# An expert layer with 96 slots on four 32-column groups of TensorE and fp32 weights that are not split

## The chip, the cores and the metric

The kernel runs on one core of a Trainium2 chip. The metric is the device time of one execution in microseconds; lower is better. The profiled execution's time and its span (first to last recorded instruction) are both given below. TensorE is called PE, its weight loads PEld, VectorE DVE, ScalarE ACT, and the queue that issues the weight transfers SP.

## What is computed

The model has two layers over 256 tokens (128 of a prompt and 128 latent). Layer 0 ends in a dense feed-forward block; layer 1 ends in eight experts of which each token uses two. D_MODEL is 1024, D_FF_EXPERT is 3584, and everything is float32.

```python
def swiglu(h, w_gate, w_up, w_down):
    return (jax.nn.silu(h @ w_gate) * (h @ w_up)) @ w_down

def moe_swiglu(h, w_router, we_gate, we_up, we_down):
    ...
    top_v, top_i = lax.top_k(logits, TOP_K)
    top_w = jax.nn.softmax(top_v, axis=-1)
    gates = jnp.sum(jax.nn.one_hot(top_i, N_EXPERTS, dtype=jnp.float32) * top_w[..., None], axis=1).astype(h.dtype)
    y = jnp.zeros_like(x)
    for e in range(N_EXPERTS):
        y = y + gates[:, e:e + 1] * swiglu(x, we_gate[e], we_up[e], we_down[e])
    return y.reshape(b, s, d)
```

One expert's three matrices hold 3 x 1024 x 3584 floats, 44.04 MB, and all eight experts are read.

## The kernel before

The layers ahead of the experts (modulation, projections, attention, pooling, dense block, router) are the same in both kernels and take the first 580 us. Then a loop, written once and run eight times on every engine, does one expert per pass.

**Slots.** The tokens of an expert are put into 128 slots by a matmul with a 0/1 matrix P (`gather`, into the tile xg), and its outputs Y are spread back over the 256 tokens and weighted by a matmul with PgT (`combine`), which DVE adds to the result (`add_up`). If an expert had more tokens than slots, a second round would follow under an `If`; with this data no expert has over 77 tokens.

**Weights.** SP loads the weights in items of 1 MB into `ring`, 7 slots of 8 KB in each of 128 partitions; an expert has 42 items. Gate and up items are 4 rows of 512 columns (2 KB each) in a partition, down items one row of 8 KB. ACT copies each half item (a piece) into `high`, rounded to the type fp32r, and DVE puts the difference into `low`; each piece is then used in three matmuls instead of one (high times high, high times low, low times high). An fp32r matmul is one hardware matmul; a plain fp32 call is two, each with its own weight load, so that a call appears in the trace as two MATMUL and two LDWEIGHTS records. The transposes are one each.

**Steps.** The 3584 hidden columns are done in 7 steps of 512. A step is `into_hidden(0, ...)` for gate (24 matmuls of 512 columns), `turn` of the step before (4 transposes), `into_hidden(1, ...)` for up (24), and `down` of the step before (24). In all an expert has 504 fp32r matmuls of 128x128 by 512 columns, 28 transposes, a gather (16 calls) and a combine (8 calls).

**Order.** Every engine has a program of its own, in the order of the code, and they meet at semaphores: SP waits for `low_ready` before it loads into a slot, ACT waits for `in_slot` and `pieces_used`, DVE for `high_ready`, PE for `low_ready`. Silu is one ACT instruction over 512 columns, the product with up one of DVE.

**Four column groups elsewhere.** The modulation (`mod_rows`, L1222) already uses 32-column matmuls on the four 32-column groups of the array, in plain fp32: eight calls, call i into partitions 32i to 32i+31 of one bank, each with its own 512 weight columns streaming:

```python
                    for i in range(4):
                        k = 4 * half + i
                        last = mm(mod_rows_of(m)[32 * i:32 * i + 32, :], silu_c[:, k, :], w[:, i, :], start=half == 0, stop=half == 1)
```

Of the kernel before, what the change touches and what calls it, by code (L numbers as in the profile page):

```python
# [18 lines left out]
D = 1024  # L19
# [14 lines left out]
NE = 8  # L34
FE = 3584
# [12 lines left out]
EC = 512  # L48
ESTEPS = FE // EC
# [4 lines left out]
E_ITEMS = 6 * ESTEPS  # L54
E_PIECES = 2 * E_ITEMS
assert E_PIECES % PIECES == 0
COMBINE_BANKS = (6, 7, 3, 2)
# [126 lines left out]
MOE_ARRIVED = list(_count)  # L184
PER_EXPERT = [len(range(s, E_ITEMS, SLOTS)) for s in range(SLOTS)]

# [4 lines left out]
def piece_g(c):  # L191
    return 0 if c == 0 else 12 * c - 4


def piece_u(c):
    return piece_g(c) + 4


def piece_d(c):
    return 12 * c + 16 if c < ESTEPS - 1 else E_PIECES - 4  # L200


def expert_item(i):

    for c in range(ESTEPS):
        for what, at in (("g", piece_g(c)), ("u", piece_u(c)), ("d", piece_d(c))):
            if 0 <= 2 * i - at < 4:
                return what, c, (2 * i - at) // 2


def program(nc, ins, consts, y_prompt, y_sample, new_ckv, new_kpe):
# [10 lines left out]
    with ctx:  # L222
# [10 lines left out]

        ring = sb("ring", 128, SLOTS, SLOT)
        high = sb("high", 128, PIECES, PIECE, dt=f32r)
        low = sb("low", 128, PIECES, PIECE, dt=f32r)
        cst = sb("cst", 128, C_COLS)
# [67 lines left out]
        hTm = sb("hTm", 128, 2, EC // 128, 128, dt=f32r)  # L305
        xg = sb("xg", 128, 2, KD, 128, dt=f32r)
        ehid = sb("ehid", 128, 2, 2, EC)
        sg, hm = ehid[:, 0], ehid[:, 1]
        h2 = sb("h2", 128, 2, D)
        P = sb("P", 128, NE + 1, 2, 128)  # L310
        PgT = sb("PgT", 128, NE + 1, 2, 128)
        Y = sb("Y", 128, D)
        Pg = sb("Pg", 128, NE, 2, 128)
# [5 lines left out]
        in_slot = [sem(f"in_slot{i}") for i in range(SLOTS)]  # L319
# [23 lines left out]
        esg_ready, eh_ready, ehT_done, ehTh_ready, ehT_ready = (sem(x) for x in ("esg_ready", "eh_ready", "ehT_done", "ehTh_ready", "ehT_ready"))  # L343
        Y_ready, cmb_done, acc_ready = sem("Y_ready"), sem("cmb_done"), sem("acc_ready")
        gat_done, xgh_ready, xg_ready = sem("gat_done"), sem("xgh_ready"), sem("xg_ready")
# [64 lines left out]
        TURNED_BANKS = (4, 5, 2, 3)  # L410
# [5 lines left out]
        def _(sp):  # L416
# [7 lines left out]
            e_down = ins["moe_w_down"].rearrange("l e (c p r) n -> (l e) c p r n", p=128, r=EC // 128)  # L424
# [35 lines left out]
            def load(e, i):  # L460

                what, c, half = expert_item(i)
                s = in_slot[i % SLOTS]
                one = slice(e, e + 1) if isinstance(e, int) else bass.ds(e, 1)
                if what == "d":
                    r = EC // 128 // 2
                    src = e_down[one, c, :, half * r:(half + 1) * r, :].rearrange("o p r n -> (o p) r n")
                    sp.dma_start(slot(i, r, D), src).then_inc(s, 16)
                else:
                    k = KD // 2  # L470
                    src = (e_gate if what == "g" else e_up)[one, :, half * k:(half + 1) * k, c * EC:(c + 1) * EC].rearrange("o p k n -> (o p) k n")
                    sp.dma_start(slot(i, k, EC), src).then_inc(s, 16)

            def rest(e, rnd):

                for i in range(SLOTS, E_ITEMS):

                    if i != SLOTS + 1:
                        sp.wait_ge(low_ready, (e + NE * rnd) * E_PIECES + (MP0 + 2 * (max(i, SLOTS + 1) - SLOTS + 1)))
                    load(e, i)  # L480

            def first_of_next(e, k):

                for i in range(SLOTS):
                    before = i + SLOTS * (PER_EXPERT[i] - 1)
                    sp.wait_ge(low_ready, k * E_PIECES + (MP0 + 2 * (before + 1)))
                    load(e, i)
# [7 lines left out]
            for i in range(SLOTS):  # L495
# [4 lines left out]
                load(0, i)  # L500
# [1083 lines left out]
```

## Time and profile before

| what | value |
|---|---|
| median of 3 runs | 1636.59 us (1634.99 to 1637.54) |
| the profiled execution | 1637.08 us |
| its span | 1635.3 us |
| PE busy in the span | 1533.9 us (94%) |
| DVE, ACT busy | 1151.7, 979.0 us |
| DMA | 464.96 MB, mean 284 GB/s |
| granted TensorE clock, mean | 0.967 |

A share of busy time is a mean over stages with different limits. The end of a matmul is modelled and overlaps the start of the next one, so the time of one in a stream is the distance from start to start, not its recorded duration; where a row joins several (xN), its length holds the last one's full duration. 

The transfers between 12 and 22 us have rows of 2 KB in a partition, those between 32 and 42 us rows of 1 KB, those of the experts four of 2 KB and two of 8 KB in every six.

### The profile page before, as it was taken

The numbers are of one execution on the slowest core, as the hardware profiler recorded it, in microseconds if no ns is written. First come the engines' busy times: TensorE is split into PE (matmuls) and PEld (weight loads), VectorE is DVE, ScalarE is ACT, GpSimd is POOL, SyncE is SP. The second block draws the span as 40 slices with busy tenths as digits, with TensorE's granted clock in tenths as the row PEclk, the third lists the DMA queues.
The fourth block names the chain that finished last, engine by engine and source line by source line (L and its number), as shares of the span: only waits on it lengthen the run. The fifth ranks groups of instructions, "written<-read, shape, count | busy, mean of one in ns | idle before, by whom it ended". The sixth has DMA issues, their size and how long they took to land.

```text
span 1635.3 us, 22872 instructions
## 1 busy us (share of the span) xinstructions
PE 1533.9 (94%) x8244; PEld 1273.6 (78%) x8244; DVE 1151.7 (70%) x1260; ACT 979.0 (60%) x1131; POOL 31.8 (2%) x62
## 2 busy tenths in 40 slices
PE   5987699999787899999999999999999999999996
PEld 3856599999665788888888888888888888888884
DVE  2433544444524588889888988888888888988893
ACT  2323444433314457767767777777777777777771
POOL 0120000000030000000000000000000000000000
PEclk8899799999899799999999999999999999999998
DMA  9556387777442459989989989989989989998960
GB/s 348 197 202 215 119 291 265 266 266 235 153 141 99 165 212 369 362 310 357 364 309 356 364 314 358 356 313 357 358 310 359 368 312 361 354 362 309 360 230 27
DMA packets 210284, 464.96 MB, mean 284 GB/s; under 512 B 9226, under 2 KB 51892, under 8 KB 195892
## 3 DMA queue, kind: packets, MB, share of 16 engines
q1 hardware_dynamic: 208324, 462.80, 78.1%
q10 hardware_dynamic: 1904, 1.41, 0.3%
q8 instruction: 35, 0.57, 0.1%
q14 instruction: 21, 0.17, 0.0%
HBM read 462.80 MB, written 1.38 MB: 284 GB/s over the span
## 4 chain that ended last, share of the span: by engine, by line
PE 91%; DVE 5%; ACT 2%; DMA 1%; issue 1%; SPq 0%; DVEq 0%; ACTq 0%
PE ps L1492 13%; PE ps L1490 13%; PE ps L1491 13%; PE ps L1513 6%; PE ps L1512 6%; PE ps L1511 6%; PE ps L1255 5%; PE ps L1257 5%; PE ps L1256 5%; PE ps L1222 2%; PE ps L1457 2%; PE ps L1266 2%; PE ps L1448 2%; PE ps L1500 2%; PE ps L1395 1%; PE ps L1397 1%
## 5 line engine op out<-in xcount | busy, mean ns | idle before, releaser
L1030 DVE TENSOR_TENSOR low<-ring,high 128x1024 fp32r<-128x1024 f32 x672 | 796.0, 1221 | 92.1 <-ACT high L730 89.2
L730 ACT ACTIVATE high<-ring 128x1024 fp32r<-128x1024 f32 x672 | 697.4, 1061 | 177.6 <-PE ps L1492 114.3
L1490 PE MATMUL ps<-high,xg 128*128 128x512 f32 x896 | 359.1, 401 | 0.0
L1492 PE MATMUL ps<-high,xg 128*128 128x512 f32 x896 | 354.5, 396 | 0.0
L1491 PE MATMUL ps<-low,xg 128*128 128x512 f32 x896 | 353.6, 395 | 0.0
L826 DVE TENSOR_TENSOR low<-ring,high 128x1024 fp32r<-128x1024 f32 x102 | 121.2, 1221 | 158.9 <-ACT high L580 158.9
L1255 PE MATMUL ps<-hx,high 128*128 128x256 f32 x640 | 186.0, 291 | 36.6 <-DVE hx L865 21.5
L1492 PEld LDWEIGHTS ps<-high,xg 128*128 128x128 f32 x896 | 168.2, 188 | 40.3
L1490 PEld LDWEIGHTS ps<-high,xg 128*128 128x128 f32 x896 | 169.0, 189 | 38.3 <-issue 0.2
L1491 PEld LDWEIGHTS ps<-low,xg 128*128 128x128 f32 x896 | 168.4, 188 | 38.6
L1257 PE MATMUL ps<-hx,low 128*128 128x256 f32 x640 | 183.8, 287 | 0.0
L1256 PE MATMUL ps<-hx,high 128*128 128x256 f32 x640 | 183.6, 287 | 0.0
L1511 PE MATMUL ps<-high,hTm 128*128 128x512 f32 x448 | 177.6, 396 | 0.0
L1513 PE MATMUL ps<-high,hTm 128*128 128x512 f32 x448 | 177.1, 395 | 0.0
L1512 PE MATMUL ps<-low,hTm 128*128 128x512 f32 x448 | 177.0, 395 | 0.0
L580 ACT ACTIVATE high<-ring 128x1024 fp32r<-128x1024 f32 x102 | 103.3, 1054 | 98.3 <-PE ps L1257 41.0
L1255 PEld LDWEIGHTS ps<-hx,high 128*128 128x128 f32 x640 | 124.5, 195 | 47.3 <-issue 36.9
L1256 PEld LDWEIGHTS ps<-hx,high 128*128 128x128 f32 x640 | 124.5, 195 | 0.0
L1257 PEld LDWEIGHTS ps<-hx,low 128*128 128x128 f32 x640 | 124.2, 194 | 0.0
L1513 PEld LDWEIGHTS ps<-high,hTm 128*128 128x128 f32 x448 | 84.1, 188 | 20.4
L1512 PEld LDWEIGHTS ps<-low,hTm 128*128 128x128 f32 x448 | 84.1, 188 | 20.1
L1511 PEld LDWEIGHTS ps<-high,hTm 128*128 128x128 f32 x448 | 84.1, 188 | 20.0
(198 smaller groups left out, 1277.7 us busy)
## 6 DMA issues: line engine op xcount, KB each, us to landing
ring<-in_moe_w_gate SPq DMA_DIRECT2D x112, 1024.0 KB, 6.5
ring<-in_moe_w_up SPq DMA_DIRECT2D x112, 1024.0 KB, 6.9
ring<-in_moe_w_down SPq DMA_DIRECT2D x112, 1024.0 KB, 6.3
ring<-in_w_ada SPq DMA_DIRECT2D x48, 1024.0 KB, 11.2
ring<-in_ffn_w_gate SPq DMA_DIRECT2D x11, 1024.0 KB, 10.8
ring<-in_ffn_w_up SPq DMA_DIRECT2D x11, 1024.0 KB, 5.5
ring<-in_ffn_w_down SPq DMA_DIRECT2D x11, 1024.0 KB, 7.3
ring<-in_w_in SPq DMA_DIRECT2D x8, 1024.0 KB, 12.0
```

The lines of the kernel that those rows point to most:

```text
L730: A(high[:, (MP0 + i) % PIECES, :], ring[:, s, half * PIECE:(half + 1) * PIECE], ACT.Copy).then_inc(high_ready, 1)
L826: V.tensor_tensor(lo, raw, hi, ALU.subtract).then_inc(low_ready, 1)
L1030: V.tensor_tensor(low[:, q, :], ring[:, n % SLOTS, half * PIECE:(half + 1) * PIECE], high[:, q, :], ALU.subtract).then_inc(low_ready, 1)
L1255: mm(out, hi[:, k, :], xh, start=k == 0, stop=False)
L1256: mm(out, hi[:, k, :], xl, start=False, stop=False)
L1257: last = mm(out, lo[:, k, :], xh, start=False, stop=k == KD - 1)
L1490: mm(ps[:, bank, :], xh, hi[:, j, :], start=kk == 0, stop=False)
L1491: mm(ps[:, bank, :], xh, lo[:, j, :], start=False, stop=False)
L1492: last = mm(ps[:, bank, :], xl, hi[:, j, :], start=False, stop=kk == KD - 1)
L1511: mm(o, xh, hi[:, 0, n], start=a, stop=False)
L1512: mm(o, xh, lo[:, 0, n], start=False, stop=False)
L1513: last = mm(o, xl, hi[:, 0, n], start=False, stop=z)
```

## The change

Only the expert layer changes. It has 96 slots (three groups of 32) instead of 128. The weights are used as they arrive, in plain fp32 calls, so nothing of `high`, `low` and their copies is left in the expert layer; `ering` lies over the memory of `ring`, `high` and `low` and has 14 slots of 8 KB. A call has 32 slots as its stationary columns and goes to one of the four 32-column groups. Gate and up of a step take four chunks of the hidden columns times three groups of slots, 12 calls per row of weights, dealt to the column groups in turn; down takes four chunks of 256 output columns times three groups of slots, in the order of DOWN_ORDER, dealt likewise. Steps are 4 x 256 columns wide three times and 4 x 128 once. Gate and up items are 2 rows of 4 KB in a partition (in the last step 4 of 2 KB), down items 8 KB, in the last step two blocks of 4 KB.

An item has 24 calls of 256 columns, in the last step's gate and up 48 of 128. An expert has 576 + 192 calls for gate and up and 336 for down, 1104 in all, and as every call is two hardware matmuls, 2208 weight loads and matmuls; it has 21 transposes, and gather and combine as before (96 columns and rows instead of 128).

Because a group of slots meets chunk after chunk on different partitions, Y is put together by five copies of ACT and three of DVE (`move_Y`). ACT has one Silu of 768 columns in a step, DVE one product of 768, and each copies half of the transposed hidden values. The loop is now one body run eight times on all engines.

```diff
--- before.py
+++ after.py
-EC = 512
-ESTEPS = FE // EC
+CAP = 96
+ESLOTS = 14
+E_STEPS = ((0, 256), (1024, 256), (2048, 256), (3072, 128))
+UP_AT = 768
+DOWN_GROUP = ((0, 1, 2), (0, 1, 3), (0, 3, 2), (3, 1, 2))
+DOWN_ORDER = ((0, 0), (0, 1), (0, 2), (1, 2), (1, 0), (1, 1), (2, 2), (2, 1), (2, 0), (3, 1), (3, 2), (3, 0))
+DOWN_BANK, TURN_BANK, GATHER_BANK = 3, 5, 0
+COMBINE_BANKS = (5, 6, 3, 4)
...
+        ering = nc.alloc_sbuf_tensor_at("ering", [128, ESLOTS, SLOT], f32, offset=ring_at)
...
+                    w = e_down_pairs if width == 256 else e_down_blocks
+                    src = w[one, col // 256 + j, :, :, :].rearrange("o p r n -> (o p) r n")
...
-                    k = KD // 2
-                    src = (e_gate if what == "g" else e_up)[one, :, half * k:(half + 1) * k, c * EC:(c + 1) * EC].rearrange("o p k n -> (o p) k n")
+                    k = SLOT // (4 * width)
+                    src = (e_gate if what == "g" else e_up)[one, :, j:j + k, col:col + 4 * width].rearrange("o p k n -> (o p) k n")
...
+            sp.wait_ge(pieces_used, MP0)
+            for i in range(SLOTS, ESLOTS):
+                load(0, i)
...
-                    A(high[:, (MP0 + i) % PIECES, :], ring[:, s, half * PIECE:(half + 1) * PIECE], ACT.Copy).then_inc(high_ready, 1)
...
+            def take_Y(k):
+                if k is not None:
+                    act.wait_ge(items_used, k)
+                lo, hi = ps[:, DOWN_BANK, :], ps[:, DOWN_BANK + 1, :]
+                A(Y[0:64, 0:512], lo[0:64, :], ACT.Copy)
+                A(Y[64:96, 0:256], lo[64:96, 0:256], ACT.Copy)
+                A(Y[0:32, 512:768], hi[0:32, 0:256], ACT.Copy)
+                A(Y[32:64, 768:1024], hi[32:64, 256:512], ACT.Copy)
+                A(Y[64:96, 512:1024], hi[64:96, :], ACT.Copy).then_inc(Y_ready, 1)
...
+                        A(sg[:, 0:3 * width], flat[:, 0:3 * width], ACT.Silu).then_inc(esg_ready, 1)
...
-                    V.tensor_tensor(low[:, q, :], ring[:, n % SLOTS, half * PIECE:(half + 1) * PIECE], high[:, q, :], ALU.subtract).then_inc(low_ready, 1)
...
+                        V.tensor_tensor(hm[:, 0:3 * width], sg[:, 0:3 * width], flat[:, UP_AT:UP_AT + 3 * width], ALU.mult).then_inc(eh_ready, 1)
+                        if s == 0:
+                            add_up(k * 4 + 4 * rnd)
...
+                pe.wait_ge(PgT_first_ready, rnd + 1)
+                pe.wait_ge(PgT_last_ready, rnd + 1)
                 with pe.Fori(0, NE) as e:
...
-                                mm(ps[:, bank, :], xh, hi[:, j, :], start=kk == 0, stop=False)
-                                mm(ps[:, bank, :], xh, lo[:, j, :], start=False, stop=False)
-                                last = mm(ps[:, bank, :], xl, hi[:, j, :], start=False, stop=kk == KD - 1)
...
+                                    for u in range(12):
+                                        (c, g), group, a = divmod(u, 3), u % 4, at + u // 4 * width
+                                        bank = (a // 512, group)
+                                        last = mm(flat[32 * group:32 * group + 32, a:a + width], xg[:, j + r, 32 * g:32 * g + 32], w[:, r, c * width:(c + 1) * width],
+                                                  start=bank not in opened, stop=j + r == KD - 1, skip_group_check=True)
...
+                                for d, g in DOWN_ORDER:
+                                    u = 3 * c + g
+                                    j = DOWN_GROUP[d][g]
+                                    last = mm(ps[32 * j:32 * j + 32, DOWN_BANK + d // 2, 256 * (d % 2):256 * (d % 2 + 1)],
+                                              hTm[:, u // 4 * h + q, u % 4 * 32:u % 4 * 32 + 32], w[:, r + q, 256 * d:256 * (d + 1)],
...
                     for s in range(NSTEP):
+                        gate_up(s)
+                        if s:
+                            down(s - 1, opened)
                         else:
...
                             combine(e)
+                            pe.wait_ge(acc_ready, k * 4 + (4 * rnd + 4))
+                        turn(s)
                     gather(e + 1)
+                    down(NSTEP - 1, opened)
...
```

PE's program at the loop's start and through the first gate pieces. `ps` is PSUM, `xg` the gathered tokens, "x23" means that 23 more of the same follow. Before:

```order
L1476 ISA
L1520 ISA [waits xg_ready]
L1481 ISA [waits esg_ready]
L1490 MATMUL ps<-high,xg 128x512 [waits low_ready]
L1491 MATMUL ps<-low,xg 128x512
L1492 MATMUL ps<-high,xg 128x512
L1490 MATMUL ps<-high,xg 128x512
L1491 MATMUL ps<-low,xg 128x512
L1492 MATMUL ps<-high,xg 128x512
L1481 REGISTER_ALU
L1490 MATMUL ps<-high,xg 128x512 [waits low_ready]
```

After, the same place:

```order
L1454 UNCONDITIONAL_BRANCH [waits PgT_last_ready,PgT_first_ready]
L1454 ISA
L1459 ISA [waits xg_last_ready,xg_first_ready]
L1475 MATMUL ps<-ering,xg 32x256 [waits in_slot0]
L1475 MATMUL ps<-ering,xg 32x256 x23
L1459 REGISTER_ALU
L1475 MATMUL ps<-ering,xg 32x256 [waits in_slot1]
L1475 MATMUL ps<-ering,xg 32x256 x23
L1475 MATMUL ps<-ering,xg 32x256 [waits in_slot2]
```

An item that was 12 matmuls of 512 columns in two pieces behind DVE's `low_ready` is now 24 calls of 256 columns that wait for the transfer itself, and the wait for both PgT copies stands ahead of the loop.

PE's program at the combine in the first step (`Y` is the output of the expert before; acc_ready comes from DVE's additions). Before:

```order
L1492 MATMUL ps<-high,xg 128x512
L1457 ISA [waits PgT_last_ready,PgT_first_ready,Y_ready]
L1457 MATMUL ps<-PgT,Y 128x256 x8
L1481 REGISTER_ALU [waits esg_ready]
L1490 MATMUL ps<-high,xg 128x512 [waits low_ready]
...
L1492 MATMUL ps<-high,xg 128x512
L1524 ISA
L1497 REGISTER_ALU [waits acc_ready]
L1500 MATMUL ps<-cst,ehid 128x128 [waits ehT_ready,eh_ready]
```

After:

```order
L1475 MATMUL ps<-ering,xg 32x256 x23
L1433 ISA [waits Y_moved,Y_ready]
L1433 MATMUL ps<-PgT,Y 128x256 x8
L1522 ISA
L1484 REGISTER_ALU [waits acc_ready]
L1487 MATMUL ps<-cst,hm 128x128 [waits eh_ready]
L1487 MATMUL ps<-cst,hm 128x128 x5
L1475 MATMUL ps<-ering,xg 32x256 [waits in_slot8]
```

Before, the 24 gate matmuls of the next step stood between the combine and the wait for acc_ready; now that wait stands directly behind the combine, with the transposes of step 0 behind it.

SP's program at the loop's start, before:

```order
L472 DMA ring<-in_moe_w_gate 128x4x512 [waits direct_used]
L472 DMA ring<-in_moe_w_up 128x4x512 [waits direct_used]
L490 UNCONDITIONAL_BRANCH
L490 ISA
L472 ISA [waits low_ready]
L472 DMA ring<-in_moe_w_up 128x4x512
```

After:

```order
L499 DMA ering<-in_moe_w_up 128x2x1024 [waits direct_used]
L499 DMA ering<-in_moe_w_gate 128x2x1024 [waits direct_used]
L499 DMA ering<-in_moe_w_up 128x2x1024 [waits pieces_used]
L499 DMA ering<-in_moe_w_gate 128x2x1024
L499 DMA ering<-in_moe_w_up 128x2x1024
...
L517 UNCONDITIONAL_BRANCH
L517 ISA
L499 ISA [waits items_used]
L499 DMA ering<-in_moe_w_gate 128x2x1024
```

Seven more items are issued ahead of the loop, and inside it a load waits for PE's last use of a slot instead of DVE's.

## Rows read from the trace of the kernel before

**Rows 1.** The page: span, busy share of the engines, chain that ended last

```profile
span 1635.3 us, 22872 instructions
...
PE 1533.9 (94%) x8244; PEld 1273.6 (78%) x8244; DVE 1151.7 (70%) x1260; ACT 979.0 (60%) x1131; POOL 31.8 (2%) x62
...
PE 91%; DVE 5%; ACT 2%; DMA 1%; issue 1%; SPq 0%; DVEq 0%; ACTq 0%
```

**Rows 2.** Windows: us, busy of PE, PEld, DVE, ACT, POOL, clock, DMA share, GB/s

```profile
590.00:717.90 127.90, 127.90 (x582) 104.77 (x581) 111.75 (x105) 96.17 (x103) 0.00 (x0) 1.00 0.93 341
...
1357.40:1485.30 127.90, 127.90 (x581) 104.61 (x581) 111.66 (x105) 96.09 (x103) 0.00 (x0) 1.00 0.94 345
```

**Rows 3.** The chain of waits from 600 to 1600, shares by line

```profile
by line: PE ps L1492 20.5%; PE ps L1491 20.4%; PE ps L1490 20.4%; PE ps L1511 10.3%; PE ps L1513 10.3%; PE ps L1512 10.3%; PE ps L1448 2.9%; PE ps L1500 2.6%; PE ps L1457 2.4%
```

**Rows 4.** Timeline of PE: start us, us, line, output<-inputs, count

```profile
582.29 0.39 PE L1491 MATMUL ps<-low,xg 128*128 128x512 f32 x1
582.52 0.39 PE L1492 MATMUL ps<-high,xg 128*128 128x512 f32 x1
```

**Rows 5.** Timeline of PE around the first gather and the second combine

```profile
704.17 0.48 PE L1511 MATMUL ps<-high,hTm 128*128 128x512 f32 x1
...
721.05 3.61 PE L1457 MATMUL ps<-PgT,Y 128*128 x16
724.32 0.58 PE L1490 MATMUL ps<-high,xg 128*128 128x512 f32 x1
```

**Rows 6.** Longest pieces of the chain from 600 to 1600: a gather

```profile
700.84 3.57 PE ps L1448 x32
```

**Rows 7.** Timeline from 579.5 to 583.4: transposes and PgT copies before the loop

```profile
579.98 1.97 PE L1474 MATMUL ps<-cst,Pg 128*128 128x128 f32 x16 [0.69 <-DVE over L1100]
...
581.98 1.29 DVE L1093 COPY PgT<-ps 128x512 f32<-128x512 f32 x2 [0.26 <-PE ps L1474]
```

**Rows 8.** Timeline of PE, four column groups: one visit

```profile
213.52 0.28 PE L1257 MATMUL ps<-hx,low 128*128 128x256 f32 x1
213.73 1.92 PE L1222 MATMUL ps<-ring,silu_c 128*32 128x512 f32 x16
215.59 0.39 PE L1255 MATMUL ps<-hx,high 128*128 128x256 f32 x1
```

**Rows 9.** Timeline of the weight loads, another visit

```profile
77.84 0.16 PEld L1222 LDWEIGHTS ps<-ring,silu_c 128*32 128x32 f32 x8
78.30 0.13 PEld L1222 LDWEIGHTS ps<-ring,silu_c 128*32 128x32 f32 x4 [0.30 <-issue]
```

**Rows 10.** DVE by form, whole span: line, shapes, count | busy, mean ns

```profile
L1114 DVE TENSOR_TENSOR sq<-sq,ps 128x512 f32<-128x512 f32 x36 | 23.2, 682 | 7.2 <-PE ps L1457 6.0
...
L850 DVE TENSOR_TENSOR sq<-xT,rs 128x1024 f32<-128x1024 f32 x8 | 9.4, 1220 | 0.1
```

**Rows 11.** ACT by form, before the router

```profile
L645 ACT ACTIVATE arena<-arena 128x768 f32<-128x768 f32 x2 | 1.7, 846 | 0.1
```

**Rows 12.** Two lines of PE's sequencer in the first expert, first and last start

```profile
L1481 PEldq ALU_OP  x3: 32/32/42, 582.0 to 582.2; - x3
...
L1527 PEldq ALU_OP  x1: 32/32/32, 583.5 to 583.5; - x1
```

**Rows 13.** Windows with a busy DMA, columns as above

```profile
12.00:22.00 10.00, 9.45 (x55) 4.96 (x53) 2.48 (x4) 2.67 (x5) 1.06 (x1) 1.00 1.05 387
32.00:42.00 10.00, 4.39 (x21) 3.93 (x19) 3.98 (x13) 6.09 (x12) 0.00 (x0) 0.50 1.10 343
610.00:690.00 80.00, 80.00 (x355) 64.96 (x354) 71.73 (x66) 62.05 (x65) 0.00 (x0) 1.00 0.99 369
```

**Rows 14.** The page: instruction fetches

```profile
q8 instruction: 35, 0.57, 0.1%
```

**Rows 15.** Timeline of the last expert's end

```profile
1605.15 0.40 PE L1513 MATMUL ps<-high,hTm 128*128 128x512 f32 x1
...
1606.72 3.72 PE L1457 MATMUL ps<-PgT,Y 128*128 128x256 f32 x16 [1.17 <-ACT Y L753]
```

More of the change, by code:

```diff
@@ L53 @@
 PIECES = 7
[L54 to L57, printed above, removed]
+CAP = 96
+ROUNDS = -(-N2 // CAP)
+ESLOTS = 14
+E_STEPS = ((0, 256), (1024, 256), (2048, 256), (3072, 128))
+NSTEP = len(E_STEPS)
+assert sum(4 * w for _, w in E_STEPS) == FE
+UP_AT = 768
[3 more added lines that the diff above has]
+COMBINE_BANKS = (5, 6, 3, 4)
 PAD = 8
@@ L183, with expert_items, gate_up, down @@
     ARRIVED.append(_count[_n % SLOTS])
-MOE_ARRIVED = list(_count)
-PER_EXPERT = [len(range(s, E_ITEMS, SLOTS)) for s in range(SLOTS)]
+MOE_ARRIVED = _count + [0] * (ESLOTS - SLOTS)
 DIRECT_USED = {("cache", 0): 1, ("uq", 0): 2, ("uq", 1): 2, ("ukv", 0): 3, ("pool", 0): 4}
[L191 to L208, printed above, removed]
+def expert_items():
+    def gate_up(s):
+        rows = 2 * 256 // E_STEPS[s][1]
+        return [(what, s, k) for k in range(0, KD, rows) for what in "gu"]
+    def down(s):
+        return [("d", s, i) for i in range(4 * E_STEPS[s][1] // 256)]
+    out = gate_up(0)
+    for s in range(1, NSTEP):
+        out += gate_up(s) + down(s - 1)
+    return out + down(NSTEP - 1)
+EXPERT = expert_items()
+E_ITEM = {x: i for i, x in enumerate(EXPERT)}
+E_ITEMS = len(EXPERT)
+GATE_UP_END = [max(i for i, x in enumerate(EXPERT) if x[:2] == ("u", s)) + 1 for s in range(NSTEP)]
+PER_SLOT = E_ITEMS // ESLOTS
+assert PER_SLOT * ESLOTS == E_ITEMS
 def program(nc, ins, consts, y_prompt, y_sample, new_ckv, new_kpe):
@@ L317, in program @@
         ps = ctx.enter_context(nc.psum_tensor("ps", [128, 8, 512], f32))
-        in_slot = [sem(f"in_slot{i}") for i in range(SLOTS)]
+        in_slot = [sem(f"in_slot{i}") for i in range(ESLOTS)]
         high_ready, low_ready, pieces_used, direct_used = (sem(x) for x in ("high_ready", "low_ready", "pieces_used", "direct_used"))
@@ L504, in _ @@
             with sp.If(more > 0):
-                first_of_next(0, NE - 1)
-                experts(1)
+                for rnd in range(1, ROUNDS):
+                    first_of_next(0, NE * rnd - 1)
+                    experts(rnd)
             sp.wait_ge(y_first_ready, 1)
@@ L803, in _ @@
             with act.If(more > 0):
-                experts(1)
+                for rnd in range(1, ROUNDS):
+                    experts(rnd)
             norm_a(2 * DEPTH)
@@ L1166, in _ @@
             with dve.If(more > 0):
-                experts(1)
+                for rnd in range(1, ROUNDS):
+                    experts(rnd)
             for k in range(KD):
@@ L1549, in _ @@
             with pe.If(more > 0):
-                experts(1)
+                for rnd in range(1, ROUNDS):
+                    experts(rnd)
             norm(2 * DEPTH)
```

270 lines of the change are left out of this document (110 added, 160 removed).

## The prediction

> **What bounds the kernel now.** The page comes first: PE is busy for 94% of the span and holds 91% of the chain that ended last [rows 1]. The windows of single experts say it more sharply: in 127.90 us PE is busy for 127.90, at clock 1.00, while DVE has 111.7, ACT 96 and the DMA share is 0.93 to 0.94 [rows 2]. The chain from 600 to 1600 us has nothing in it but PE's lines [rows 3]. So an expert costs what PE streams, and the split on ACT and DVE is hidden, though not by much.
>
> PE's time closes. A 512-column fp32r matmul starts 0.23 us after the one before, exactly 0.2325 when the rest is taken off [rows 4]: 504 of them are 117.2 us. The combine takes 724.32 - 721.05 = 3.3 us [rows 5], the gather 704.17 - 700.84 = 3.3 [rows 5, 6], 28 transposes at 1.97 / 16 = 0.12 [rows 7] 3.4. That is 127.2; 0.7 is left for the loop's branch and register work.
>
> **The groups of four.** The new form stands in the trace already, at L1222. Four weight loads of 32 columns come together and the next four 0.43 to 0.46 us later, 77.84 to 78.30 [rows 9]; sixteen hardware matmuls take from 213.73 to about 215.5 [rows 8]. So four fp32 matmuls of 512 columns on the four column groups cost 0.43 us together, what one alone would. The combine gives the price for 256 columns from another side: 16 in 3.3 to 3.6, 0.205 to 0.216 each [rows 5, 15]. I take half of 0.429, 0.2145, for four of 256 columns. An expert has 2 x (576 + 336) = 1824 of them, 456 fours: 97.8 us.
>
> The last step's 384 hardware matmuls of 128 columns are 96 fours. By columns each would be 0.107. But four weight loads last 0.13 [rows 9], so 0.13 is the more cautious price, and no row shows loads and streams at this pace. I take 0.12: 11.5 us, bounds 10.3 and, if the pace of the 256-column form is a floor, 20.6.
>
> **The rest of a pass.** 21 transposes 2.5, combine 3.3, gather 3.3 (96 columns for 128 on the moving side could save 0.8, which I leave as margin), branch and registers 0.7. PE changes between column groups and the whole array four times. One visit in the trace: from the last ordinary start at 213.52 to the next at 215.59 are 2.07 us, of which 0.12 are the ordinary matmul and 1.72 the four fours [rows 8, 9]; 0.25 to 0.3 are left. 4 x 0.3 = 1.2.
>
> **The moved wait.** PE now waits for acc_ready directly behind the combine, before the transposes. DVE's four additions of 0.68 [rows 10] stand behind its product of 768 columns, which I put at 0.95, between the 0.68 of 512 and the 1.22 of 1024 [rows 10], and that behind ACT's Silu of 768 columns, 0.85 [rows 11]. From the last up matmul on: 0.85 + 0.95 + 4 x 0.68 = 4.5, with about 0.4 for three hand-overs 4.9. The combine covers 3.3 of it; 1.5 us of PE stand still, queued behind them the transposes and gate of step 1, for which nobody else waits yet. Before, 24 matmuls, 5.6 us, lay between. If it is hidden after all the term is 0, if the combine's last quarter must be waited for too, 2.
>
> All: 97.8 + 11.5 + 2.5 + 3.3 + 3.3 + 0.7 + 1.2 + 1.5 = 121.8 us against 127.9.
>
> **Work that goes off PE's neighbours.** ACT loses 84 copies and DVE 84 subtractions per expert. That is worth nothing by itself, since neither is in the chain [rows 3]. The copies of xg lie under the last down items (24 fours, 5.1 us), those of Y under the next expert's first gate and up items, 41 us.
>
> **Supply.** 44.04 MB in 121.8 us asks for 362 GB/s, where 341 to 345 flow now [rows 2]. These are no limit, since PE sets the pace. Where the queue was kept full it moved 387 with rows of 2 KB, 343 with rows of 1 KB, and within the expert stage 369 over 80 us [rows 13]. Rows of 4 and 8 KB should not be worse than the mix of 2 and 8. So a transfer-bound expert would be 44.04 / 387 = 113.8 to 44.04 / 369 = 119.3 us: just under PE's 121.8, with 14 MB of ring, a third of an expert, to smooth it. I count 0. The Trainium skill ("DMA: Bandwidth & Descriptors", Specifications) gives about 358 GB/s of HBM for one core; by it an expert would be 123.0 us and the sum 10 us higher. The trace's 387 and 369 speak against that as a ceiling here.
>
> **Start and end.** The loop cannot start before both PgT copies are in, 581.98 + 1.29 = 583.27 against 581.96 [rows 7]; smaller P, Pg give a little back: +1. At the end Y needs five ACT copies where two lay in the 1.6 us between the last down matmul and the last combine [rows 15]: 2 x 0.6 + 3 x 0.42, less their overlap, +1.3.
>
> **Sum.** 8 x (127.9 - 121.8) = 48.8 saved, 2.3 added, from the profiled 1637.1 (0.5 above the median): 1590.6, as a median 1590.
>
> **Rivals.** *PE bound, as worked out*: one expert between 119.5 (the last step's fours at 0.107, 0.2 instead of 0.3 a switch, half the stall: 1.2 + 0.4 + 0.7 less) and 124.3 (456 fours at 0.22 instead of 0.2145). Its own range, 8 x these, is 1572 to 1611. Chance 0.52.
>
> *Supply binds.* For it: the needed 362 is a hair below the best long stretch, and DMA shares of 0.99 there leave nothing; the instruction stream is four times as long (2208 pairs of load and matmul besides the small stages, where 504 stood) and may have to be fetched anew in each pass, through the same engines. Against: the full queue's 387, and fetches that are 35 packets and 0.1% of the span now [rows 14]. At 355 GB/s an expert is 124 us, at 345 127.7: 1608 to 1637, which takes in "no change". Chance 0.22.
>
> *PE is fed too slowly: slower than before.* Pairs of load and matmul come every 0.0536 us in fours of 256 columns and every 0.027 in those of 128; before, every 0.23. If there is a floor f per pair, the 256-column form hides it up to 0.0536; the 384 pairs of the last step then cost 384 f. The sum of the rest is 121.8 - 11.5 = 110.3, so it decides at f = 17.6 / 384 = 0.046 us. For it: the densest sustained stream in the trace is L1222's at 0.107 per pair. Against: the sequencer passed two L1481 instructions 12 pairs apart within 0.2 us, 582.0 to 582.2, less than 0.02 per pair, while the queue filled; up to L1527 at 583.5 it took 24 pairs in 1.6 us, at most 0.067, but then the queue was full and held it back [rows 12]. With f = 0.0536 an expert is 130.9 and the kernel 1663; with 0.067, 148 + 12.5 = 160 and 1900. Chance 0.16. The skill ("TensorE: Matmul & The Clock Gate", Part 2, step by step) has a rule for this: with hardware decoding off, the sequencer spends about 62 ns per MATMUL, and by it 2208 of them are 137 us, an expert 149 and the kernel about 1810. The row of L1481 contradicts it, as do the starts of L1222, if such a burst tells of a long stream.
>
> *Cheaper than worked out*: with no stall, no switches and 0.8 less for the gather 121.8 - 1.2 - 1.5 - 1.2 - 0.8 = 117.1, 1552 us; 1552 to 1572 has 0.10. That the slots need a second round is excluded by the 77 tokens at most.
>
> **How the numbers follow.** A measurement of this kernel tells 0.2%, 3.3 us, from no change. Faster is the first and last case and most of the supply one, 0.52 + 0.10 + 0.17 = 0.79; same 0.05; slower 0.16. The range of 1566 to 1638 leaves out the slow case and part of the cheapest.
>
> **What would show it.** In windows of one expert: 121.8 us apart, PE busy throughout but 1.5 us before the first transposes of a pass, clock 1.00, DMA near 362. Four loads and four matmuls of L1475 0.2145 apart; in the last step 0.107 to 0.13. If supply binds, PE's idle stands before L1475 with a DMA as its releaser; if feeding binds, it stands before it with "issue" and the distance in the last step is near that of the others. Idle PE could also lower the granted clock, which in this stage has been 1.00 [rows 2]; with pauses of 1.5 us I expect none of that.

## The result, and the profile after

The changed kernel takes 1648.41 us (median of 5, 1645.94 to 1653.58) against 1637.12 (1634.99 to 1639.79) for the kernel before on the same chip: ratio 1.0072, interval 1.0051 to 1.0092. It is slower by 0.5 to 0.9%, where 1590 us was forecast. Its profiled execution has a span of 1646.7 us.

The page of the changed kernel, its head and its chain, answering to [rows 1], and the instruction fetches, answering to [rows 14]:

```profile
span 1646.7 us, 46591 instructions
...
PE 1491.8 (91%) x21820; PEld 1096.5 (67%) x21820; DVE 333.2 (20%) x555; ACT 274.7 (17%) x429; POOL 31.8 (2%) x62
...
q8 instruction: 188, 3.08, 0.7%
...
PE 86%; DVE 6%; issue 4%; ACT 2%; DMA 1%; SPq 1%; ACTq 0%; DVEq 0%
```

PE is busy for 42 us less than before, and yet the span is 11 us longer. What came up in the chain is "issue", which means that an engine waited for nothing that the profile shows. The instruction queue (q8) went from 35 packets to 188.

Windows of one pass of the changed kernel (us, busy of PE, PEld, DVE, ACT, POOL, clock, DMA share, GB/s), for [rows 2]:

```profile
734.70:864.60 129.90, 122.43 (x2282) 82.14 (x2279) 9.31 (x16) 7.90 (x14) 0.00 (x0) 0.99 0.89 342
```

A pass has 129.9 us, of which PE is busy for 122.4, where 121.8 and "busy throughout but 1.5" were forecast. The list of PE's waits from 590 to 1600 us (who waited for what: us in total, times, longest) names two:

```profile
PE ps L1475 <- issue: 47.1, 18, 5.1
PE ps L1487 <- DVE sq L1113: 6.8, 8, 0.9
```

The second is the moved wait, 0.86 us a pass. The first is 47 us in 18 pieces. The timeline of PE shows the two kinds of piece, one at the loop's branch and one in the last step, and the moved wait between them (in brackets the idle time before a row):

```profile
705.12 2.13 PE L1504 MATMUL ps<-ering,hTm 128*32 128x256 f32 x36
712.32 4.06 PE L1475 MATMUL ps<-ering,xg 128*32 128x256 f32 x42 [5.07 <-issue]
...
739.24 0.98 PE L1487 MATMUL ps<-cst,hm 128*128 128x128 f32 x6 [0.86 <-DVE sq L1113]
...
804.42 4.55 PE L1475 MATMUL ps<-ering,xg 128*32 128x128 f32 x155
810.53 6.66 PE L1475 MATMUL ps<-ering,xg 128*32 128x128 f32 x227 [1.56 <-issue]
```

And this is what PE's sequencer did at the loop's branch, first in the kernel before (L1476), then in the changed one (L1454); duration in ns as least, median and greatest:

```profile
L1476 PEldq COMPARE_BRANCH  x8: 76/208/256, 705.8 to 1601.3; - x8
```

```profile
L1454 PEldq COMPARE_BRANCH  x8: 83/5938/6118, 705.9 to 1615.1; - x8
```

The branch that took 0.2 us takes 5.9; only the last of the eight, which is not taken, is still short. Behind the pause the clock falls: the window of 3.4 us after it, beside a later one of the same length.

```profile
712.30:715.70 3.40, 3.38 (x36) 1.69 (x40) 0.00 (x0) 0.00 (x0) 0.00 (x0) 0.55 0.06 19
716.00:719.40 3.40, 3.40 (x68) 1.94 (x64) 0.00 (x0) 0.00 (x0) 0.00 (x0) 1.00 0.42 100
```

At the granted clock of 0.55 (nearly all of it at the level of 1.2 GHz) 36 matmuls run where 68 do at full clock; that is about 1.5 us lost in a pass. The clock was 0.50 to 0.60 behind all seven pauses.

What was forecast of the matmuls came in. A stretch of 384 matmuls of 256 columns in the changed kernel, from the chain's longest pieces:

```profile
642.25 20.86 PE ps L1475 x384
```

20.86 us for 96 fours (a four: four matmuls, one on each column group), with the end of the last one 0.217 each, from start to start 0.216; forecast 0.2145. The list of waits names no transfer.

The last step pauses in seven passes and not in the eighth. From its first matmul to its last it takes 12.6 to 13.1 us in the seven, with a pause of 1.8 to 2.0 us (from start to start) in front of matmul 156 and a second of 0.3 to 0.6 in front of matmul 284. In the eighth, when the last weights have arrived, it takes 10.5:

```profile
1586.01 10.68 PE L1475 MATMUL ps<-ering,xg 128*32 128x128 f32 x382
```

```profile
1585.00:1590.00 5.00, 5.00 (x158) 4.79 (x158) 0.42 (x1) 0.60 (x1) 0.00 (x0) 1.00 0.01 3
```

The two places are 128 matmuls apart. A pass of 2277 matmuls, the pass that begins at 706 us, brings 19 instruction packets of 16 KB, about 120 pairs of load and matmul in each besides other instructions, so 128 is the distance of two packets in dense code. An item of weights is 96 pairs here, so a wait for weights would come at multiples of 96.

### The profile page after: what moved, and what is told of

Same layout as the page of the kernel before. It is cut to its first block, busy times and chain, and to the rows that moved or that the text cites. A ratio compares the mean times of both kernels' runs of the same rounds, so it can differ in the third digit from the quotient of the medians.

```text
span 1646.7 us, 46591 instructions
## 1 busy us (share of the span) xinstructions
PE 1491.8 (91%) x21820; PEld 1096.5 (67%) x21820; DVE 333.2 (20%) x555; ACT 274.7 (17%) x429; POOL 31.8 (2%) x62
## 4 chain that ended last, share of the span: by engine, by line
PE 86%; DVE 6%; issue 4%; ACT 2%; DMA 1%; SPq 1%; ACTq 0%; DVEq 0%
PE ps L1475 37%; PE ps L1504 18%; PE ps L1231 5%; PE ps L1233 5%; PE ps L1232 5%; PE ps L1198 2%; PE ps L1242 2%; PE ps L1424 2%; PE ps L1487 2%; PE ps L1371 1%; PE ps L1373 1%; PE ps L1372 1%; PE ps L1208 1%; PE ps L1433 1%; DMA ring<-in_w_ada 1%
## 5 line engine op out<-in xcount | busy, mean ns | idle before, releaser
L1475 PE MATMUL ps<-ering,xg 128*32 128x256 f32 (+1 forms) x12288 | 604.0, 357 | 49.1 <-issue 47.1
L1475 PEld LDWEIGHTS ps<-ering,xg 128*32 128x32 f32 x12288 | 381.5, 111 | 264.5 <-issue 68.5
L1504 PE MATMUL ps<-ering,hTm 128*32 128x256 f32 x5376 | 298.3, 379 | 0.0
L1504 PEld LDWEIGHTS ps<-ering,hTm 128*32 128x32 f32 x5376 | 204.5, 110 | 84.7 <-issue 1.2
L829 DVE TENSOR_TENSOR low<-ring,high 128x1024 fp32r<-128x1024 f32 x102 | 121.3, 1223 | 159.3 <-ACT high L612 159.3
L612 ACT ACTIVATE high<-ring 128x1024 fp32r<-128x1024 f32 x102 | 103.4, 1054 | 98.4 <-PE ps L1233 41.3
L1198 PE MATMUL ps<-ring,silu_c 128*32 128x512 f32 x384 | 49.1, 635 | 1.6 <-DMA ring<-in_w_ada 1.6
L1371 PE MATMUL ps<-fx,high 128*128 128x256 f32 x176 | 50.4, 286 | 0.0
L1373 PE MATMUL ps<-fx,low 128*128 128x256 f32 x176 | 49.6, 282 | 0.0
L1372 PE MATMUL ps<-fx,high 128*128 128x256 f32 x176 | 49.5, 281 | 0.0
L1433 PE MATMUL ps<-PgT,Y 96*128 (+1 forms) x144 | 35.2, 400 | 2.5 <-ACT Y L779 2.5
```

The source lines that it names most:

```text
L612: A(next(halves(q, raw)), raw, ACT.Copy).then_inc(high_ready, 1)
L829: V.tensor_tensor(lo, raw, hi, ALU.subtract).then_inc(low_ready, 1)
L1371: mm(o, hi[:, 0, mc], xh, start=a, stop=False, skip_group_check=True)
L1372: mm(o, hi[:, 0, mc], xl, start=False, stop=False, skip_group_check=True)
L1373: last = mm(o, lo[:, 0, mc], xh, start=False, stop=z, skip_group_check=True)
L1475: last = mm(flat[32 * group:32 * group + 32, a:a + width], xg[:, j + r, 32 * g:32 * g + 32], w[:, r, c * width:(c + 1) * width], start=ban ...
```

## The experiments

The theory (F) after the traces were read: the loop's body, 2277 pairs of load and matmul instead of 580, is no longer kept by PE's sequencer, so each pass is fetched anew; a taken branch waits for the first fetch, and the densest stretch outruns the fetches. The rivals: the pauses are waits for weights or xg; they belong to the branch or to the dense code whatever its length; or fetching limits straight code as well.

### PE's loop written out eight times

```diff
-                with pe.Fori(0, NE) as e:
+                def expert(e):
                     k = e + NE * rnd
...
+                    for e in range(NE):
+                        expert(e)
```

> The changed kernel with PE's loop over the experts written out eight times, so that PE has no backward branch; all other engines keep their loops. Theory F (a pass is fetched anew, and at the branch PE waits for the first fetch of the pass): the seven pauses of 5.0 to 5.5 us between the last down matmul and the first L1475 go, and with them the 1.5 us at half clock behind each; 7 x 6.6 = 46 us less, time about 1602; the pause of 1.8 us in the last step of each pass stays. Rival S (the pauses are waits for weights or for the xg copies that end at the same place): nothing changes, 1648. Rival L (straight code is fetched no faster than a loop's, and the fetches are what costs): pauses of the same sum elsewhere, 1640 to 1648.

Measured: 1609.77 us (1601.95 to 1617.92), ratio to the kernel before 0.9824 (0.9772 to 0.9876). The seven pauses are gone, and passes are 123.0 to 125.1 us apart instead of 129.7 to 131.5. The last steps still pause, mostly for 1.3 to 2.8 us, some a second time for 0.6 to 2. F holds; rivals S and L fall. 39 us came back where 46 were expected: the seven last steps that pause are 4.4 us longer in sum, and the last combine ran at a lower clock and took 1.7 us more.

With the loop written out, the passes no longer begin at the same place of a packet, and the first pause moves from pass to pass (in front of matmul 163, 187, 210, 234, 257 of the step), while a second one, where there is one, is mostly 128 matmuls behind the first:

```profile
925.04 5.97 PE L1475 MATMUL ps<-ering,xg 128*32 128x128 f32 x209
932.49 3.70 PE L1475 MATMUL ps<-ering,xg 128*32 128x128 f32 x128 [1.48 <-issue]
937.88 1.41 PE L1475 MATMUL ps<-ering,xg 128*32 128x128 f32 x44 [1.69 <-issue]
```

So these pauses belong to the packets of code and neither to a place in the kernel nor to an item of weights.

### Two experts in a body of the changed kernel

```diff
-                with pe.Fori(0, NE) as e:
+                def expert(e):
...
+                with pe.Fori(0, NE // 2) as pair:
+                    expert(pair * 2)
+                    expert(pair * 2 + 1)
```

> The changed kernel with two experts in a body of PE's loop, four passes: 3 backward branches that are followed by more work instead of 7. Theory F: the pause goes with the branch, 4 x 6.6 = 26 us less, about 1622. If the pause goes with the expert (its first wait for xg or for weights), 1648.

Measured: 1625.99 us (1623.33 to 1628.52), ratio 0.9934 (0.9918 to 0.9951). Distances between the combines alternate, 125.3, 130.3, 123.3, 129.9, 123.5, 129.3, 123.1: the long pause is there after every second expert only. It goes with the branch, at 6.1 us a branch by the mean distances (129.9 against 123.8) and 5.6 by the medians, where 6.6 was expected.

### Long bodies in the kernel before

```diff
-                with pe.Fori(0, NE) as e:
+                def expert(e):
...
+                with pe.Fori(0, NE // 4) as group:
+                    for i in range(4):
+                        expert(group * 4 + i if i else group * 4)
```

> The kernel before with PE's loop of eight passes turned into two passes of four experts each: 4 x 580 = 2320 pairs of load and matmul, about the length of the changed kernel's body (2277), but with one pair every 0.23 us. Theory F (bodies of this length are not kept and the branch waits for a fetch): the branch record of 76 to 256 ns becomes 5 to 6 us once (there is one backward branch less than two passes), fetches go on through the whole stage instead of the first expert only (some 190 instruction packets instead of 35), and the time rises by 4 to 6 us, to about 1642. If only the density of the 32-column form makes the pause: no change, 1637, branch at 0.2 us.

> The kernel before with two experts in a body of PE's loop, four passes: 1160 pairs, about 148 KB of instructions. Tells where between 580 and 2277 pairs a body stops being kept. If kept: about 10 instruction packets more than before, no pause, 1637. If not: three pauses of 5 us and fetches in every pass, 1650.

(With two experts in a body it is `NE // 2` and `range(2)`.) Measured: 1637.65 us with four experts in a body and 1637.84 with two, ratios 1.0006 (0.9993 to 1.0019) and 1.0002 (0.9985 to 1.0019). Neither changed the time, and both expectations were half right. The branch and the fetches of the version with four, then the branch of that with two:

```profile
q8 instruction: 72, 1.18, 0.3%
```

```profile
L1542 PEldq COMPARE_BRANCH  x2: 83/1823/3563, 1090.5 to 1602.2; - x2
```

```profile
L1542 PEldq COMPARE_BRANCH  x4: 83/3620/3783, 842.9 to 1610.6; - x4
```

The taken branch takes 3.6 us instead of 0.2 and packets rise from 35 to 72 and 77, so already 1160 pairs are not kept, while 580 are. (I had expected 190 packets; two passes of 2320 pairs at 128 pairs in a packet are 36 more.) But PE did not pause. The timeline of PE in the version with four, during its branch of 1090.5 to 1094.1:

```profile
1090.89 0.40 PE L1513 MATMUL ps<-high,hTm 128*128 128x512 f32 x1
1091.13 0.39 PE L1511 MATMUL ps<-high,hTm 128*128 128x512 f32 x1
...
1093.23 0.40 PE L1511 MATMUL ps<-high,hTm 128*128 128x512 f32 x1
```

PE works on what is queued: 15 or 16 matmuls at 0.2325 us start during each of the four long branches of these two versions, up to 3.4 to 3.6 us behind the branch's start, and the next follows without a gap. In the changed kernel 20 matmuls start during the branch, but at 0.054 us each they are done with after 1.0 us, and PE stands still until the branch is over: 5.9 - 1.0 + 0.4 = 5.3 us from start to start. So the same stall of the sequencer is hidden behind long matmuls and open behind short ones. The long body alone cost nothing here, with the DMA idle at the branch (below); that the dense form with a body short enough to be kept would cost nothing either was not run, it is inferred from the 0.2 us of a body of 580 pairs.

### What the fetch waits for: half the traffic, then nearly none

```diff
+                part = 1 if isinstance(e, int) else 2
...
-                    sp.dma_start(ering[:, i % ESLOTS, :].rearrange("p (k n) -> p k n", k=k), src).then_inc(arrives, 16)
+                    sp.dma_start(ering[:, i % ESLOTS, 0:SLOT // part].rearrange("p (k n) -> p k n", k=k // part), src[:, 0:k // part, :]).then_inc(arrives, 16)
```

> The changed kernel where in the first seven experts the loads inside the loop bring only the first half of each item (the second half of a slot keeps older data, so the expert layer's outputs are not the reference's): the DMA moves half as much while the code is the same. If the fetches are slow because the weights fill the DMA engines, the pause at the branch falls from 5.4 to 2 or 3 us and that in the last step from 1.8 to under 0.5: 30 us less or more, about 1615. If the fetch has a time of its own, both stay within 0.5 us of 5.4 and 1.8, about 1645. If supply of weights were the bound after all, the whole pass would shorten by more than the pauses.

```diff
...
+                    n = 4 * width if isinstance(e, int) else 128
+                    sp.dma_start(ering[:, i % ESLOTS, :].rearrange("p (k n) -> p k n", k=k)[:, :, 0:n], src[:, :, 0:n]).then_inc(arrives, 16)
```

> The changed kernel where in the first seven experts the loads inside the loop bring only 128 columns of each row (the rest of a slot keeps older data, so the expert layer's outputs are not the reference's); code and order the same, DMA nearly idle. Theory Q (a fetch of instructions has a time of its own of about 3.5 us at the branch, and waits behind weights that are under way for the rest): the branch record falls to 3.3 to 3.7 us, the pause there to about 3.0, the pause in the last step goes; a pass of about 124.5 us, time about 1608. Rival N (the 5.9 us are what a branch out of a dense PE program costs, whatever the DMA does): branch 5 to 6, pass 128 to 130.

Measured, one run each: 1628.51 us with half the traffic, 1606.18 with nearly none. With half of it the pauses at the branch were 3.1 to 4.0 us and those in the last step 0.3 to 1.0, between the two forecasts; with nearly none, theory Q's figures came in. The branch in both:

```profile
L1455 PEldq COMPARE_BRANCH  x8: 83/4478/4958, 705.5 to 1595.1; - x8
```

```profile
L1456 PEldq COMPARE_BRANCH  x8: 82/3516/3905, 702.6 to 1572.8; - x8
```

And the last step of the second, whole:

```profile
797.11 10.69 PE L1477 MATMUL ps<-ering,xg 128*32 128x128 f32 x384
```

With little traffic (a DMA share of 0.26 during the branch) it takes 3.5 us, and the last step's 96 fours take 10.69 us without a pause, 0.11 each. So of the changed kernel's 5.9 us at the branch 3.5 are the fetch's own and 2.4 come from the weights' traffic, and the whole pause of the last step does; the changed kernel's own eighth pass says the same of the last step.

The packets of the traces show where the 2.4 us lie. In each of these branches one instruction packet of 16 KB is fetched, and it takes about 1.0 us with traffic (0.96 to 1.02) and without (0.93 to 1.12); the branch ends some 1.4 us behind it. What differs is when the packet starts: 1.0 to 1.5 us behind the branch's start with nearly no traffic, 1.8 to 2.2 with half of it and 3.2 to 3.8 in the changed kernel. The time is lost before the packet's transfer, not in it.

The kernel before with long bodies fits in: at each of its four long branches the DMA happened to be idle (share 0.00 to 0.02), and in the changed kernel it was not. Windows of the version with four experts in a body, then of the changed kernel:

```profile
1091.00:1095.00 4.00, 4.00 (x19) 3.21 (x18) 4.00 (x6) 3.39 (x5) 0.00 (x0) 1.00 0.04 8
```

```profile
706.00:712.00 6.00, 1.25 (x24) 0.51 (x16) 1.28 (x3) 2.30 (x5) 0.00 (x0) 1.00 0.90 336
```

With nearly no traffic, passes are 123.5 and 125.2 us, in turn, against 130 (the longer ones have a stretch at a granted clock of 0.60, 4 us long, behind the branch's pause of 2.5 us; in the passes between, behind pauses of 2.5 to 3.0, it is 1.00): that is what remains of the changed kernel when only the fetch's own 3.5 us stand at each branch.

### Shorter packets, fewer slots

```diff
...
+                    for h in range(PARTS[i]):
+                        sp.dma_start(to[:, :, h * n:(h + 1) * n], src[:, :, h * n:(h + 1) * n]).then_inc(arrives, 16)
```

> The changed kernel with each gate and up item of 256-column steps loaded by two transfers of 2 KB rows instead of one of 4 KB rows (bytes, slots and order the same; down keeps 8 KB). So far the branch record was 3.6 us in the kernel before with long bodies (2 and 8 KB rows), 5.9 in the changed kernel (4 and 8 KB), 4.5 with half its traffic. Theory P (a fetch waits behind the weights' packets, and longer behind longer ones): the branch falls to about 4 us, the pause to 3.5, the one in the last step to about 1; 7 x 2 + 8 x 0.8 = 20 us less, 1628. Rival U (what counts is how full the DMA is, not the size of packets: the kernel before asked for 341 GB/s too, but PE there never waited for its code): the branch stays within 0.4 of 5.9, time 1645 to 1650, or more, since 2 KB rows keep the engines busier.

> The version with all three edits (1597) with the same 2 KB rows. Theory P: the pauses of 0.5 to 2 us that remain in each pass (some 2.5 us a pass) shrink by half, 8 to 12 us less, about 1587. Rival U: 1595 to 1605.

Measured: 1657.46 us (1653.35 to 1664.69), ratio 1.0109 (1.0064 to 1.0154), branch 5.2 to 6.1 us; in the version with all edits 1599.58 against 1597.34 with long rows, ratios 0.9752 and 0.9753. Theory P, that a fetch waits longer behind longer packets, falls. Whether 2 KB rows cost anything is not clear, as the interval of 1.0109 overlaps that of the changed kernel's 1.0072.

```diff
-                        sp.wait_ge(items_used, (e + NE * rnd) * E_ITEMS + ((joined if i == joined - 1 else i) - ESLOTS + 1))
+                        sp.wait_ge(items_used, (e + NE * rnd) * E_ITEMS + ((joined if i == joined - 1 else i) - ESLOTS + 1 + 5))
...
-                    sp.wait_ge(items_used, k * E_ITEMS + (E_ITEMS - ESLOTS + i + 1))
+                    sp.wait_ge(items_used, k * E_ITEMS + (E_ITEMS - ESLOTS + i + 1 + 5))
```

> The changed kernel with each load inside the loop waiting for five more items to be used: in effect a ring of 9 slots, so that fewer transfers stand in the DMA's queues when a fetch comes. If the depth of the queue makes the fetch long: branch 4 to 5 us, the pauses shorter, 5 to 10 us less than the changed kernel. If the ring's depth does not matter, 1645 to 1650; if 9 slots are too few to ride over the DMA's own dips, waits for weights appear and it is over 1655.

> The same later loads in the version with PE's loop written out and the split wait (1597.6): under the first theory 1590 to 1595, with no effect 1597, with waits for weights over 1600.

Measured: 1651.02 us (1649.3 to 1653.19), ratio 1.0077 (1.0058 to 1.0097), branch 5.5 to 5.8 us; written out 1601.32 (1595.74 to 1602.78), ratio 0.9768 (0.9742 to 0.9794). Against the 1.0072 and 0.9756 of the same versions with 14 slots neither is a difference. The depth of the ring is not what makes the fetch long, and 9 slots do as well as 14.

### The moved wait, and the order in the last step

```diff
-                            pe.wait_ge(acc_ready, k * 4 + (4 * rnd + 4))
+                            pe.wait_ge(acc_ready, k * 4 + (4 * rnd + 2))
                         turn(s)
...
+                        if s == 1:
+                            pe.wait_ge(acc_ready, k * 4 + (4 * rnd + 4))
```

> The changed kernel with one wait in two: behind the combine PE waits for two of DVE's four additions (those of the banks that the transposes write), and for all four before the first down. If the 1.24 us between the combine's last matmul and the first transpose are that wait, as the trace says, about 0.9 to 1.0 us go in each pass: 7 to 8 us less, time about 1641. If PE would have waited there for the product's transposes input anyway, under 2 us.

Measured: 1644.96 us (1642.87 to 1651.07), ratio 1.0041 (1.0026 to 1.0056). The idle time before the transposes is gone from the profile, 0.9 us a pass, but the passes are only 0.6 us shorter (129.7 in the mean against 130.2): a part is lost again in other pauses (PE's waits with "issue" are 48.9 us instead of 47.1). It is worth 3 to 5 us.

```diff
-    for s in range(1, NSTEP):
+    for s in range(1, NSTEP - 1):
         out += gate_up(s) + down(s - 1)
+    g, d = gate_up(NSTEP - 1), down(NSTEP - 2)
+    out += g[:2] + d[:2] + g[2:] + d[2:]
```

> The changed kernel with the last step's gate and up items (matmuls of 128 columns, a four every 0.109 us) alternating two by two with the down items of the step before (a four every 0.216). Theory D (the 1.8 us pause in the last step comes where 128 instruction pairs are used up in 3.5 us, faster than a fetch returns): each dense stretch is half as long, 192 pairs, and the pause shrinks to under 0.5 or goes: 8 x 1.3 to 1.8 = 10 to 14 us less, about 1636. Rival (the pause belongs to the place in the code, or to the weights' transfer): it stays at 1.8, time 1648.

Measured: 1655.45 us (1652.74 to 1657.67), ratio 1.0107 (1.0076 to 1.0139), not the gain that theory D forecast; the interval overlaps that of 1.0072, so a loss isn't clear either. The pause stays, 1.5 to 2.4 us, at the same place, 155 dense matmuls into the step: half a dense stretch, 192 pairs, is still longer than the 128 pairs of one fetch. The mixing was too coarse to test density; that the dense stretch alone does not pause without traffic is shown by the run with tiny loads and by the changed kernel's eighth pass.

### The edits together

> The changed kernel with the three edits together: PE's loop written out, two of the four additions waited for before the transposes, and the last step's gate and up items between the down items of the step before. If the three pauses are independent the gains add: 46 + 7 + 12 = 65 us less than the changed kernel, about 1583, a pass of 121.5 us; then the transfers at 44.04 MB in 121.5 us, 362 GB/s, may begin to bind, and with that rival it stays at 1590 to 1600.

> The changed kernel with the loop of PE written out and the split wait for the additions, without the mixing of the last step: tells what the mixing is worth once the branch is gone. By the sum of the single runs 1609.8 - 3.5 to 7 = 1603 to 1606, and then the mixing gives 6 to 9 us in the version with all three, though alone it cost 7; if the mixing is worth nothing, 1597.

> The version with all three edits and 2 KB rows, and the waits for the two PgT copies moved from ahead of the loop to the first combine, where they were before. The gap from the last transpose to the first L1475 was 1.7 to 2.2 us, 0.4 before: 1.3 to 1.7 us less than the same without it. If the first L1475 is held by its code or the xg copies, no change.

Measured: all three edits 1597.34 us (1596.18 to 1598.07), ratio 0.9753 (0.9736 to 0.9769); loop written out and split wait without the mixing 1597.64 (1594.06 to 1609.44), 0.9756 (0.9702 to 0.981); all three with 2 KB rows and the later PgT waits 1598.21, 0.9752 (0.9719 to 0.9786). These times cannot be told apart, so the mixing, the rows and the PgT waits are worth nothing that shows in them. The trace does show the PgT waits: PE's 1.4 us of waiting for a PgT copy ahead of the loop are gone, the gain that was expected, though it is no more than the scatter of the runs. The sum of the three single gains (1583) was not reached, as the mixing gave none; and 1590 to 1600 came out, but not for that rival's reason, since PE's waits in the version with all three are 15.7 us of "issue" and none for a transfer. The simplest version, with the loop written out and the split wait, is 2.4% faster than the kernel before (by the interval 1.9 to 3.0%) and about 3% faster than the changed one. One of its usual passes, and one of the quick ones:

```profile
729.40:852.90 123.50, 120.39 (x2278) 80.54 (x2278) 9.30 (x16) 7.91 (x15) 0.00 (x0) 1.00 0.94 359
1222.80:1345.00 122.20, 120.26 (x2278) 82.59 (x2278) 9.29 (x16) 7.89 (x15) 0.00 (x0) 1.00 0.95 363
```

PE is busy for 120.3 us of a pass; 2 to 3 us are pauses, most of them in the last step. The DMA carries 359 and 363 GB/s here.

## Why the prediction was wrong, by its own steps

**The fours: right.** 0.216 to 0.217 us measured, 0.2145 predicted; the last step's 0.109 to 0.11, predicted 0.12, bounds 0.107 and 0.215.

**"0.7 is left for the loop's branch and register work": the step that failed.** The remainder of the old kernel's pass was carried over as if a branch cost the same after any body. It took 0.2 us there because a body of 580 pairs is kept, and that much was hidden behind the matmul in flight. In the changed kernel the record is 5.9 us and the pause, from start to start, 5.0 to 5.5, with 1.5 us lost at about half clock behind it: 7 x 6.7 = 47 us. The Trainium skill ("Runtime: NRT & Kernel Launch", Instruction fetch mechanics) says that TensorE's instruction memory holds 2048 instructions, that it is refilled in sequence in 16 KiB blocks, and that a taken branch out of what is held must wait for a fetch. The runs agree: 580 pairs, 1160 instructions, are kept, 1160 pairs are not, and the branch then takes 3.5 us or more. That rule spoke against the change, and it was not weighed.

The price could have been read from the trace of the kernel before as well. Behind its loop stands the `If` of the second round, whose branch jumps over that round's code, and with an idle DMA it took 3.3 us, most of them hidden behind the last combine:

```profile
L1549 PEldq COMPARE_BRANCH  x1: 3304/3304/3304, 1607.3 to 1607.3; - x1
```

**The supply rival saw the second fetch and asked the wrong question.** It said that the code may have to be fetched anew in each pass, and looked at it only as load on the DMA engines: about 155 packets in the stage, 0.7% of the engines' time for all 188, harmless indeed. The cost is in the latency, where a branch or a dense stretch waits for one packet.

**The feeding rival** named the right engine and the right side (slower than before), but as a floor per pair that decides at 0.046 us. No such floor is there: without traffic the 384 pairs of the last step run at 10.69 / 384 = 0.028 us each. Under the weights' traffic that step takes 12.6 to 13.1 us, 0.033 to 0.034 each, in the form of one pause or two. This is the second term that the sum put at nothing: 7 x 2.4 = 17 us. By the 62 ns per MATMUL that the Trainium skill states for hardware decoding off ("TensorE: Matmul & The Clock Gate", Part 2) an expert would have been 149 us; this case's rows deny it.

**Small terms.** The moved wait: 1.5 predicted, 0.9 to 1.0 measured. Start: +1 predicted, 583.70 against 581.96, +1.7 (the last PgT copy ends at 583.13, and 0.6 is the entry into the loop). End: the gap between the last down matmul and the last combine 1.57 and 2.85 us, +1.3 as predicted; not foreseen was that the last combine then runs at a lower clock (0.68 against 1.00), +1.7. Behind that combine the changed kernel is 2.5 us quicker to its end, and the cause of that stays open. The visit that priced a change of column groups leaves 2.07 - 0.12 - 1.72 = 0.23 us, not 0.25 to 0.3.

**Supply: right.** PE never waited for weights in the expert stage, with up to 363 GB/s over a pass of the best version. The 358 GB/s that the Trainium skill gives ("DMA: Bandwidth & Descriptors", Specifications) were passed and did not bind.

The account: 1590.6 + 47 for the branches + 17 for the pauses of the last steps = 1654.6. The terms that came out smaller, in each of eight passes 1.0 for the last step's fours and 0.5 for the moved wait, less 0.7 for 456 fours at 0.216, take 6.4 off. Start and end are + 0.7 + 1.7 - 2.5. That is 1648.1; the profiled execution took 1648.5.

What stays open is by which way the weights' traffic delays a fetch. The delay lies before the packet starts, and it changes neither with the size of the weights' packets nor with the number of slots; what the fetch waits for in that time no run shows. A last step with finer mixing, the 32-column form in a body of under 580 pairs, and a long body of the kernel before with a busy DMA at its branch were not tried.

## What to carry to other kernels

Before matmuls are made smaller and more numerous inside a loop, count the pairs in the body: past the length that the sequencer keeps (between 580 and 1160 pairs here), each taken branch costs 3.4 to 6.1 us, of which only what is queued on the engine hides anything, and small matmuls queue little time. Look at the duration of COMPARE_BRANCH and at the count of instruction packets of the kernel before, and ask what they would be with the new length. Look also for branches of the kernel before that already leave what is kept. Writing the loop out for PE alone turned 0.7% slower into 1.8% faster, and with the split wait 2.4%.

## What the runs showed of the hardware that was not expected

- A body of 580 pairs of weight load and matmul is kept by PE's sequencer, one of 1160 is not; the taken branch then takes 3.4 to 3.9 us with a quiet DMA, 4.1 to 5.0 with half the traffic and 5.2 to 6.1 with all of it.
- During the branch one instruction packet of 16 KB is fetched, in 0.9 to 1.4 us with and without traffic. In the changed kernel this packet starts 3.2 to 3.8 us behind the branch's start instead of 1.0 to 1.5 with a quiet DMA.
- Pairs on four column groups run at 0.028 us each over 384 pairs when little or nothing else uses the DMA. When the weights flow, such a stretch pauses for about 1.8 us, and a second pause comes 128 pairs behind the first.
- After a pause of 5 us the granted clock was 0.55 in the next 3.4 us, nearly all at 1.2 GHz; with pauses of 2.5 to 3.0 us the clock fell (to 0.60 over 4 us) in every second pass only.
